# Token-major x and B by VectorE block transposes, and the second modulation's column sums taken by VectorE

## What is computed

```python
mod_l = (silu(c) @ w_ada + b_ada)              # 6 x 1024: shift/scale/gate 1, shift/scale/gate 2
h = modulate(rmsnorm(x), shift1, 1 + scale1)
z, xbc, dt, g_b, g_c, v = split(h @ w_in)      # xbc: x (1024), B (4 x 128), C (4 x 128)
xbc = silu(conv5(xbc) + conv_b)                # along the tokens, each channel for itself
dt = softplus(dt + dt_bias); a = -exp(a_log) * dt
# chunks of 128 tokens, forward and backward, 16 heads of 64 in 4 groups:
acs = cumsum(a)                                # over a chunk's tokens
states = einsum('bclgn,bclgr,bclgrp->bcgrpn', B, exp(acs_end - acs), x * dt)
y = y_diag + y_off                             # from C, B, x, the decays and the states
x1 = x + gate1 * rmsnorm(concat(norm(y * silu(z)), norm(g_b * conv3(g_c * v))) @ w_out)
h2 = modulate(rmsnorm(x1), shift2, 1 + scale2)
out = x1 + gate2 * rmsnorm(peer(h2))           # 8 heads, top 16 of 16384 experts each
```

## Time and profile before

| | us |
|---|---|
| runs, median of 3 | 1884.4 (1882.55 to 1885.38) |
| the profiled execution: its time | 1884.75 |
| the profiled execution: its span | 1882.9 |
| busy: PE, VectorE, POOL, ScalarE | 1435.3, 1451.5, 855.5, 547.1 |

### The profile page before, as it was taken

How to read it: one execution, slowest core, us unless ns; L and a number is a source line. 1 busy time by engine, 2 the same in 40 slices (tenths; PEclk the granted TensorE clock), 3 DMA queues, 4 the chain that set the end, 5 groups by cost and what they waited for, 6 DMA issues and landing times.

```text
span 1882.9 us, 15679 instructions
## 1 busy us (share of the span) xinstructions
PE 1435.3 (76%) x4503; PEld 830.9 (44%) x4503; DVE 1451.5 (77%) x2808; ACT 547.1 (29%) x1558; POOL 855.5 (45%) x626
## 2 busy tenths in 40 slices
PE   7999999999878888887787677677655554655554
PEld 2565687788545555554454234334311111211111
DVE  1545359773797779888967898889989889898877
ACT  3100233432332334223322432233322222222222
POOL 0888410010454443443434455446656555555551
PEclk9999999999989988999889898779878777777876
DMA  9534311343999999999999999999999999999995
GB/s 382 192 147 152 116 65 55 108 176 135 379 393 421 422 421 421 422 421 422 420 421 420 385 399 421 421 423 421 421 421 422 420 422 422 422 422 421 422 422 246
DMA packets 91228, 652.52 MB, mean 347 GB/s; under 512 B 10494, under 2 KB 10886, under 8 KB 12806
## 3 DMA queue, kind: packets, MB, share of 16 engines
q0 software_dynamic: 76448, 555.78, 71.6%
q1 hardware_dynamic: 13808, 93.39, 12.5%
q10 hardware_dynamic: 887, 2.35, 0.3%
HBM read 649.37 MB, written 2.11 MB: 346 GB/s over the span
## 4 chain that ended last, share of the span: by engine, by line
DMA 41%; PE 28%; DVE 20%; issue 6%; ACT 4%; POOL 1%; SPq 0%; DVEq 0%; ACTq 0%; POOLq 0%
DMA arena<-in_peer_uv,arena 40%; PE bank L834 12%; DVE arena L2038 8%; PE bank L1135 4%; DVE arena L2074 4%; PE bank L1023 3%; DMA arena<-in_w_ada 2%; PE bank L871 1%; POOL arena L766 1%; PE bank L948 1%; PE bank L1056 1%; ACT arena L1475 1%; PE bank L974 1%; PE bank L960 1%; DVE arena L2001 1%
## 5 line engine op out<-in xcount | busy, mean ns | idle before, releaser
L766 POOL DMA_INDIRECT arena<-in_peer_uv,arena x512 | 698.1, 1363 | 732.4 <-DVE arena L2074 451.8
L1135 PE MATMUL bank<-arena,smalls 128*128 128x512 f32 x1036 | 660.2, 772 | 419.5 <-ACT smalls L1483 419.4
L2038 DVE CUSTOM_DVE_ANT_0 arena<-arena 128x1024 f32<-128x1024 f32 x512 | 619.1, 1222 | 153.5 <-DMA arena<-in_peer_uv,arena 152.1
L1135 PEld LDWEIGHTS bank<-arena,smalls 128*128 128x128 f32 x1036 | 218.4, 229 | 781.1 <-ACT smalls L1483 589.1
L2074 DVE SCALAR_TENSOR_TENSOR arena<-arena 128x1024 f32<-128x1024 f32 x247 | 315.7, 1278 | 38.9 <-ACT arena L1475 36.3
L834 PE MATMUL bank<-arena 128*128 128x256 f32 (+1 forms) x1216 | 332.0, 430 | 2.2 <-ACT arena L1200 1.5
L1470 ACT ACTIVATE arena<-arena 128x2 f32<-128x2 f32 x255 | 51.9, 203 | 924.7 <-DVE arena L2038 924.6
L834 PEld LDWEIGHTS bank<-arena 128*128 128x128 f32 x1216 | 232.9, 193 | 102.4 <-issue 77.6
L1475 ACT ACTIVATE arena<-arena 128x1 f32<-128x1 f32 x510 | 122.5, 287 | 8.5
L1078 PE MATMUL bank<-arena 128*128 128x256 f32 x480 | 108.8, 380 | 0.0
L1483 ACT ACTIVATE smalls<-ident,arena 128x128 f32<-128x128 f32 x259 | 103.6, 401 | 8.3
(11 more groups left out here) (275 smaller groups left out, 1320.9 us busy)
## 6 DMA issues: line engine op xcount, KB each, us to landing
arena<-in_w_in SPq DMA_DIRECT2D x40, 1024.0 KB, 7.7
arena<-in_w_ada POOLq DMA_DIRECT2D x16, 1024.0 KB, 5.1
arena<-in_w_out SPq DMA_DIRECT2D x16, 1024.0 KB, 9.3
arena<-in_peer_w_q SPq DMA_DIRECT2D x16, 1024.0 KB, 9.3
arena<-in_w_ada SPq DMA_DIRECT2D x8, 1024.0 KB, 12.1
arena<-in_peer_uv,arena POOLq DMA_INDIRECT x512, 19.6
arena<-in_x SPq DMA_DIRECT2D x4, 512.0 KB, 11.9
arena<-in_x_t SPq DMA_DIRECT2D x1, 2048.0 KB, 16.0
```

The costliest lines, as they stand in the source:

```text
L766: nc.gpsimd.indirect_dma_start(gslot[slot], None, uv_tab[0], bass.IndirectOffsetOnAxis(eid[t % 2][:, k:k + 1], 0)).then_inc(s_gsl[slot], 16)
L1135: last = mm(acc[h][:, :], diag[:, k % NDG], row_v(n)[:, h * 512:(h + 1) * 512], start=first, stop=last_one)
L2038: V.tensor_tensor_reduce(row_u(n), row_u(n), h2[t], 1.0, 0.0, ALU.mult, ALU.add, dots[:, k:k + 1]).then_inc(s_dot, 1)
```

## The change

PE's 72 transposes, the 18 PSUM banks that held their results and the 18 copies out of them go. Instead VectorE turns 32x32 blocks from SBUF to SBUF (`turn_blocks`): for a pair of channel tiles, and for the latent or the context tokens, 16 instructions of 32 partitions each, one for each pair of a source block row `a` and a destination block row `b`. One instruction covers 2 channel tiles and 4 chunks (latent, 256 elements in each partition) or 2 chunks (context, 128). There are 6 pairs, so 96 instructions of each kind. `TURN` says behind which convolution each set of 16 stands; the last three context sets follow the last convolution.

The partition sums of the second modulation are now made by VectorE as a reduction over blocks of 32 with a transpose (`ada_piece`, 128x512 in, 8 times), and one PE matmul with the matrix `fold` adds the four partition blocks for all 4096 columns at once (`"ada2"`); four additions on 32 partitions bring in the bias. POOL's buffer is released by `s_ared`. On PE `"acs"` and `"m2T"` move ahead of the last z quarter, and on ScalarE that quarter's Silu moves behind the exponentials. PE's wait for `N_XTR` (all 192 block transposes) stands before the first item of `SCHED`.

```diff
-        if ct % 2 and ct > 1:
-            plan.append(("ada2", ct // 2 - 1))
-    plan += ["dtl", "dtc", ("ada2", NXB // 2 - 1), ("z", 0, 0), "dt"]
-    plan += [("z", hq, 0) for hq in range(1, 4)]
-    plan += [("xsT", m, h) for m in range(NT) for h in range(2)] + [("bT", m) for m in range(NT)]
-    plan += ["acs", "m2T"]
+    plan += ["dtl", "dtc", ("z", 0, 0), "dt", "ada2"]
+    plan += [("z", 1, 0), ("z", 2, 0), "acs", "m2T", ("z", 3, 0)]
...
                 if i == 0 and g >= 2:
-                    await_filled(pool, ("ada2", g - 2))
+                    pool.wait_ge(s_ared, g - 1)
...
+                    ps = claim("ada2")
+                    pe.wait_ge(s_fold, 1)
+                    pe.wait_ge(s_ared, NXB // 2)
+                    filled(mm(ps[:, 0:P], fold, apart, start=True, stop=True), "ada2")
+                if hq == 2:
+                    pe.wait_ge(s_a, 1)
...
             pe.wait_ge(s_xb, NXB + NCTX)
...
-            await_read(pe, ("bT", NT - 1))
+            pe.wait_ge(s_xtr, N_XTR)
...
             def ada_piece(g):
 
...
+                dve.wait_ge(s_asum, g + 1)
+                V.tensor_reduce(out=apart[:, 16 * g:16 * g + 16], in_=asum[:, g % 2].rearrange("p (b r) -> p b r", r=32),
+                                axis=mybir.AxisListType.X, op=ALU.add, apply_transpose=True).then_inc(s_ared, 1)
+
+            def turn_blocks(pair, ctx):
+
+                dve.wait_ge(s_xb, 4 * pair + 4)
+                src = xbc_c if ctx else xbl
+                ct = 2 * pair
+                dst, col = (xs, ct * P) if ct < NX else (Bt, (ct - NX) * P)
+                lo, hi = (LT, NT) if ctx else (0, LT)
+                for a in range(NBLK):
+                    for b in range(NBLK):
+                        i = src[32 * a:32 * a + 32, ct:ct + 2].rearrange("p k (m t) -> p k m t", t=P)
+                        o = dst[32 * b:32 * b + 32, lo:hi, col:col + 2 * P].rearrange("p m (k c) -> p k m c", c=P)
+                        V.transpose(o[:, :, :, 32 * a:32 * a + 32], i[:, :, :, 32 * b:32 * b + 32]).then_inc(s_xtr, 1)
+
+            TURN = {ct: [(ct // 2 - 1, 0)] for ct in range(3, NCTX + 2, 2)}
+            TURN |= {NCTX: [(0, 1)], NXB - 2: [(1, 1)], NXB - 1: [(2, 1)]}
...
                 if ct % 2 and ct > 1:
                     ada_piece(ct // 2 - 1)
-
-
+                for pair, ctx in TURN.get(ct, ()):
+                    turn_blocks(pair, ctx)
+
+            ada_piece(NXB // 2 - 1)
+            for pair in range(3, NCTX // 2):
+                turn_blocks(pair, 1)
             dve.wait_ge(s_vec, 48)
             ps = await_bank(dve, "dt")
...
-            for m in range(NT):
-                ps = await_bank(dve, ("xsT", m, 0))
-                release(V.tensor_copy(xs[:, m, 0:512], ps[:, :]), ("xsT", m, 0))
```

More of the change, by code:

```diff
@@ L387, in build @@
         asum = at(152, 2, 2 * WCOL)
+        NBLK = P // 32
+        apart, fold = at(157, 4 * KD * NBLK), at(157.5, P)
         xst = [at(k, D) for k in (188, 192, 96)]
@@ L835, in project_T @@
                 filled(last, name)
-            def ada_sum(g):
-                ps = claim(("ada2", g))
-                pe.wait_ge(s_asum, g + 1)
-                for j in range(4):
-                    last = mm(ps[:, j:j + 1], asum[:, g % 2, j * P:(j + 1) * P], ones[:, 0:1],
-                              start=True, stop=True)
-                filled(last, ("ada2", g))
             for n in range(XBC // WCOL):
@@ L1221, in _, with z_gate @@
             A(alog[:], alog[:], ACT.Exp).then_inc(s_dtl, 1)
-            for hq in range(4):
+            def z_gate(hq):
                 ps = await_bank(act, ("z", hq, 0))
@@ L1225, in _ @@
                         ("z", hq, 0))
-            for m in range(NT):
-                ps = await_bank(act, ("xsT", m, 1))
-                release(A(xs[:, m, 512:1024], ps[:, :], ACT.Copy), ("xsT", m, 1))
-            for m in range(NT):
-                ps = await_bank(act, ("bT", m))
-                release(A(Bt[:, m, :], ps[:, :], ACT.Copy), ("bT", m))
+            for hq in range(3):
+                z_gate(hq)
             act.wait_ge(s_acs, 1)
@@ L1622, in tap @@
                 return V.scalar_tensor_tensor(out=d, in0=s, scalar=w, in1=d, op0=ALU.mult, op1=ALU.add)
+            dve.wait_ge(s_const, 1)
+            V.tensor_reduce(out=fold.rearrange("p (a c) -> p a c", a=NBLK),
+                            in_=ident[:].rearrange("p (a c) -> p c a", a=NBLK).unsqueeze(1).to_broadcast([P, NBLK, 32, NBLK]),
+                            axis=mybir.AxisListType.X, op=ALU.add).then_inc(s_fold, 1)
             def ada_piece(g):
[L1626 to L1629 removed]
+                dve.wait_ge(s_asum, g + 1)
[14 more added lines that the diff above has]
+            TURN |= {NCTX: [(0, 1)], NXB - 2: [(1, 1)], NXB - 1: [(2, 1)]}
             for ct in range(NXB):
@@ L1658, in _ @@
                       "dt")
-            ada_piece(NXB // 2 - 1)
-            await_read(dve, ("ada2", NXB // 2 - 1))
+            ps = await_bank(dve, "ada2")
+            for q in range(NBLK):
+                lanes = slice(32 * q, 32 * q + 32)
+                add = V.tensor_tensor(modr[lanes, :], ps[lanes, 0:P].rearrange("p (i q) -> p i q", q=NBLK)[:, :, q],
+                                      colB[lanes, B_BA + 2 * KD:B_BA + 6 * KD], ALU.add)
+                if q < NBLK - 1:
+                    post(add)
+            release(add, "ada2")
+            settle()
+            await_read(dve, "ada2")
             link(V.tensor_scalar(modr[:, 2 * KD:3 * KD], modr[:, 2 * KD:3 * KD], 1.0, None, ALU.add))
```

46 lines of the change are left out of this document (14 added, 32 removed).

## The result

| | before | changed |
|---|---|---|
| median, us (11 runs each) | 1883.72 (1882.10 to 1885.46) | 1890.39 (1887.51 to 1896.98) |
| ratio, 95% interval | 1 | 1.0041 (1.0033 to 1.0049) |
| span of the profiled execution | 1882.9 | 1893.2 |

The changed kernel is slower by 6.7 us in the medians (1.0035); the ratio of 1.0041 is estimated from all runs, and its interval stands for 6.2 to 9.2 us.

The account below looks back on a forecast made before the run. PE, with no gap worth naming before its first state step at 257.62 us, was taken as the bound. That step 3.9 us later plus 1.6 us of clock loss gave 1884.75 + 5.5 = 1890.3 us, range 1875.5 to 1897.

Parts of the forecast that it names:

- The bound: PE ahead of its first state step at 257.62 us: a microsecond taken there should move everything behind it equally.
- What PE saves: Ahead of the first state step: 6.6 us of column sums and 7.9 of transposes, about 14 us if VectorE were in time.
- The cost of a block transpose: On VectorE: 0.448 us latent and 0.314 us context from start to start, without overlap.
- The middle value: Block transpose cost between low bounds 0.335 and 0.20 us and high bounds 0.52 and 0.38, with 0.033 us of fill.
- Rival (a): VectorE's block transposes are short or overlap: decays at 235.4 us, time 1876, or 1874 without the clock loss; chance 0.32.
- VectorE's calendar: Work fits up to tile 10; from tile 11's convolution VectorE has a queue, so the decays come at 250.0 us.
- PE's side: PE waits some 10 us for the decays, then needs 11.5 us: first state step at 261.5 us, +3.9 us.
- the clock's term: PE leaves its wait at a lower clock and loses 1.6 us on the last z quarter.
- POOL: Its buffer is released by VectorE's reduction; last group ready at 216 or 217 us, reduction due at 225, no cost.
- The time: Whole kernel: 1884.75 + 5.5 = 1890.3 us.
- rival (d): Block transposes dearer still; from about 0.52 us latent, pairs exceed PE's 20.75 us; +15 us or more, 1900; chance 0.09.
- the move of the decay sums: On PE, decay sums and the transpose of `mod2` go ahead of the last z quarter; said to only change places.

Follow-up runs that it names:

- e6: Changed kernel with all 72 transposes given back to PE, column sums still on VectorE; 1876.73 us, ratio 0.9965 to the kernel before.
- e4: Changed kernel with the context tokens' 24 tiles turned by PE, only the latent ones by VectorE; 1873.65 us, ratio 0.9943 to the kernel before.
- e8: Changed kernel with every block transpose cut in two along the channel tiles; 1899.39 us in one run.
- e3: Changed kernel with ten extra, unread PE products ahead of the wait for the decays; 1888.71 us, ratio 1.0031 to the kernel before.
- e10: Changed kernel run once more, unedited; 1888.80 us in one run.
- e9: Kernel before with only the new order, decay sums and `mod2` transpose ahead of the last z quarter; 1884.00 us, ratio 1.0004.
- e2: Changed kernel with the last z quarter ahead of the decay sums again, its Silu ahead of the exponentials; 1884.22 us, ratio 1.0003 to the kernel before.
- e5: Changed kernel with the modulation's column sums made by PE again, block transposes and new order kept; 1894.04 us, ratio 1.0058 to the kernel before.

## Why the prediction was right, point by point

**The bound.** Right: what stands ahead of the first state step passes through to the end. From the step to the end of the span are 1625.3 us before and 1623 to 1630 in the other profiles of this study, while the step itself moved between 245.0 and 268.0.

**What PE saves.** The 14 us that VectorE in time would have given were not run as such. e6 shows the column sums' part (6 us of step) and e4 both parts but for the 24 context tiles (12.6 us of step). With the 2.6 us of these tiles that is 15.2 us, an estimate, where 14 were forecast.

**The cost of a block transpose.** The step of the sum with the largest unknown came out close: 0.448 and 0.314 us were forecast, 7.40/16 = 0.463 and 5.30/16 = 0.331 came. The middle value between the neighbours' rows, with the fill of 32 elements, was right to 6%, a little low. That they do not overlap was argued from the change of partitions, and e8 shows it as the cause: with the partitions unchanged the next starts 0.07 us before the first is done (0.24 against a busy time of 0.30), with a change it starts 0.03 us behind the end. The rule of the Trainium skill that the prediction cited ("VectorE: DVE Perf Modes", "Two Vector instructions with no wait between them") holds in this case. It was tested for a change of the destination block; a change of the source block alone was not. The figure of 311 ns for a 128x128 in bf16 (same page, "The three transpose paths") stands next to 301 ns for the same number of elements in a partition here. Rival (a) failed at this step: it needed the overlap or shorter instructions.

**VectorE's calendar.** Tile 11 started its convolution at 171.79 (172.0 forecast); the decays came at 251.13 (250.0). Behind tile 11 there are 128 block transposes of 0.015 to 0.017 us more each, 2.1 us; four reductions at 0.63 us from start to start where 0.75 was taken give 0.5 back, and the start of tile 11 another 0.2. The dt chain took 9.4 us (9.3).

**PE's side.** The wait (9.02 us, some 10 forecast), the hidden waits ahead of it and the order of what follows came as forecast. The wait is shorter since the two middle z quarters, 14.0 us in the sum, took 15.70. The step that was mis-sized is the clock's term, right in kind and at the low end in size: 1.6 us were taken from the window of the kernel before, 1.5 to 3.0 came (e3 against three profiles). The window that it was taken from is not the same in every execution either: 0.59 in the kernel before, 1.00 in e10. Of the 3.0 in the first profile 0.9 are the decay sums, 1.9 us in place of 1.0, which the sum had left out, and 2.1 the z quarter. The sum had the step at 261.5 + 1.6 = 263.1; the three profiles have 265.55, 262.19 and 264.64.

**POOL.** Right: no wait for it appears in the queue, and its last group was ready at 215.4 (216 or 217 forecast), 9.7 us before its reduction. In e6, where VectorE is early, its last reduction waits for POOL until 212.91, the 213 that the prediction named, and that wait is hidden.

**The time.** 1890.3 us forecast, 1890.39 measured. So close a hit is luck, for three reasons. The change itself was forecast at 5.5 us and measured at 6.7 (6.2 to 9.2 by the interval); the sum stood on a profiled execution of 1884.75, and the median of the kernel before is 1883.72, which made up for 1.0 of it. The bounds for a block transpose put the decays anywhere from 14.6 us below to 8.6 above the 250.0 of the sum (128 times the distance to each bound), and the middle was an argued pick. And the executions of the changed kernel spread over 9.5 us.

**A slip in rival (d).** A pair fits PE's 20.75 us as long as 10.8 + 0.75 + 16 times the cost does, which is up to 0.575 us and not 0.52. e8, with 0.523 us a step, fits. Nothing in the forecast rests on it.

**What was not seen.** The prediction called the move of the decay sums neutral ("only change places"), and e9 confirms this for the kernel before. Its sum did put the z quarter's 7.0 us behind the decays, but did not ask what the old order would give. With VectorE late the move costs 6 us (e2 against the changed kernel), since 7 us of PE work stand behind the wait in place of ahead of it. Nor did the prediction ask which part of the change loses: without the context's block transposes the rest is good for 10 us (e4).

## What to carry to other kernels

Work moved to an engine with idle time pays only where that idle time is: draw up the receiving engine's calendar to the point where somebody waits for it, and put what another engine waits for ahead of what it does not. Here VectorE's idle time took the latent block transposes and the reductions, some 50 us, for nothing (e4), and the 32 us for the context tokens behind them cost all that the change had saved and 7 us more. Keep independent work of the waiting engine ahead of a wait that may come late (e2), and count a PE wait of 9 us together with the half clock that follows it.

## What the runs showed of the hardware

- A float32 block transpose on 32 partitions took 433 ns for 256 elements in each partition and 301 ns for 128. With a change of partitions between neighbours the next starts some 0.03 us after the end; without one, 0.07 us before it (e8).
- A reduction of 128x512 over blocks with a transpose takes 704 ns, like the plain one of the same size (686 ns in the earlier trace rows), and gives sums over 32 partitions.
- Behind a PE wait of 8.5 to 9.0 us a z quarter that takes 7.07 us at the upper level took 7.65, 8.01 and 9.15 us in three executions of one kernel. Behind 12.06 and 13.56 us it took 9.26 (e8) and 8.86 (e5).
